# A mixture-of-experts stage whose experts are ranked by their count of tokens, with passes of 96 and 32 rows

## The chip, the cores and the metric

The kernel runs on one core of a Trainium2 chip. The metric is the device time of one execution in microseconds (us). Everything is float32; the matrix products of the experts are plain float32 matmuls.

## What is computed

The program is a stack of transformer layers. What matters here is the routed feed-forward layer, which occurs twice (layer l = 0 and 1), on 256 tokens of width 1024. The router picks for each token one group of four experts and two experts in that group, so 512 (token, expert) pairs fall on 16 experts:

```python
def hier_moe(x, w_rg, b_rg, w_re, b_re, w_gate, w_up, w_down):
    g_prob = jax.nn.softmax((t @ w_rg).astype(jnp.float32) + b_rg, axis=-1)
    g_val, g_idx = lax.top_k(g_prob, 1)
    ...
    e_val, e_idx = lax.top_k(e_logits, EXPERT_TOPK)
    e_w = jax.nn.softmax(e_val, axis=-1)
    ...
    for g in range(G):
        hg = jax.nn.silu(jnp.einsum('td,edf->tef', t, w_gate[g])) * jnp.einsum('td,edf->tef', t, w_up[g])
        y = y + jnp.einsum('tef,efd->td', hg * combine[:, g, :, None], w_down[g])
```

Each expert has three weight tiles of 2 MB (gate, up: 1024x512; down: 512x1024). The reference's router, evaluated on the inputs that setup_inputs() draws, gives these counts of tokens for experts 0 to 15:

| layer | counts |
|---|---|
| 0 | 46 53 20 25 31 60 39 24 14 43 50 29 16 20 13 29 |
| 1 | 11 8 4 13 77 33 111 69 27 33 14 24 18 17 20 33 |

## The kernel before

**Passes.** The chosen tokens of an expert are gathered into rows of a 128-row block. A pass handles one block, which two experts share: expert 2p has rows 0 to 63 and expert 2p + 1 rows 64 to 127. Eight passes (0 to 7) cover the sixteen experts with 64 rows each. An expert with more than 64 tokens gets further "items" of 64 rows, appended behind; two items share a pass. The number of passes, `pairs`, is half of (16 + items), rounded up, and is computed on the chip (`pairs_i`). With the counts above layer 0 has 8 passes. In layer 1 expert 4 needs one item, expert 6 one and expert 7 one: three items, 10 passes.

**One pass on TensorE** (`pair`): 32 program matmuls at L1607 for gate and up (8 slices k of the width, two products, two experts), `scatter` of the previous pass (L1589, 16 matmuls), four transposes (L1653), `gather` of the next pass's tokens (L1600), and 16 program matmuls at L1607 for down. The helper `both` issues at each step k one matmul for rows 0 to 63 and one for rows 64 to 127. The stationary operand is the tokens (64 columns), the moving one 512 columns of the expert's weights, so the two matmuls use two halves of the array's columns. Each program matmul in float32 appears in the trace as two weight loads and two matmuls. I call one (64, 64) pair of program matmuls a k-step; a pass has 8 + 8 + 8 = 24.

**VectorE and ScalarE** turn the products: `hs` = silu(gate) * up (L2795, once a pass, right behind up), the one-hot tables for the next gather (L2726, L2730), and the scaled result (L2809).

**The weights** come through eight slots of 2 MB: 0 to 5, and slots 6 and 7 (named `ahead_a` and `arena` in the trace), which hold the gate tiles of every other pass. SyncE (SP) issues the loads in the order gates of pass p + 1, up of p, down of p; each waits until TensorE has read what is in the slot (`pe_read`). The loads of passes 0 to 6 have addresses that are known when the program is built (L978). From pass 7 on they are in a loop whose addresses come from `expert_i` (L1000, L1006). The loads of the first eight tiles are issued before the layer's routing is known.

**Routing** is a chain of small VectorE instructions (`experts(l)` of the vector engine, L2681 to L2732), each waiting for the one before (`link`). It gives every chosen pair its row (`gp`), the one-hot table `oh`, on which TensorE's first gather waits, and, later, `pairs_i` and `expert_i`.

Of the kernel before, what the change touches and what calls it, by code (L numbers as in the profile page):

```python
# [31 lines left out]
I32 = mybir.dt.int32  # L32
# [5 lines left out]
P = 128  # L38
# [25 lines left out]
for _name, _w in [("ident", 128), ("ones", 128), ("blk64", 128), ("rotq", 128), ("dup0", 128), ("rot0", 128),  # L64
                  ("dup1", 128), ("rot1", 128), ("rotm", 128), ("before", 128), ("iota", 128), ("cosb", T0),
                  ("sinb", T0), ("maskt", TW), ("decay", RET_H * REAL), ("cosr", REAL), ("sinr", REAL), ("cosm", REAL),
                  ("sinm", REAL), ("causal", 384), ("over", OVER), ("first64", EXPERTS), ("over64", EXPERTS),
                  ("pairs", PAIRS), ("part", 1), ("last", 2), ("ones48", 48), ("sooner", 16), ("place", 8), ("thirds", 3),
                  ("windows", PAIRS + 1)]:
    CONST[_name] = (_at, _at + _w)  # L70
    _at += _w
# [18 lines left out]
def constants():  # L90
# [4 lines left out]
    def put(name, a):  # L95
        c[:, CONST[name][0]:CONST[name][1]] = a
# [46 lines left out]
    put("thirds", np.broadcast_to(HALF * np.arange(1, 4), (P, 3)))  # L143
    put("windows", np.broadcast_to(P * np.arange(PAIRS + 1), (P, PAIRS + 1)))
    put("over", np.broadcast_to(np.arange(OVER), (P, OVER)))
    put("first64", np.broadcast_to(HALF * np.arange(EXPERTS), (P, EXPERTS)))
    put("over64", np.broadcast_to(HALF * (EXPERTS - 1 - np.arange(EXPERTS)), (P, EXPERTS)))
    put("pairs", np.broadcast_to(2 * np.arange(PAIRS), (P, PAIRS)))
    put("part", p)
    put("last", np.broadcast_to(np.array([EXPERTS - 2, EXPERTS - 1]), (P, 2)))  # L150
    put("ones48", 1.0)

    rel = np.arange(-(T0 - 1), T0)
# [7 lines left out]
def program(nc, A, out, dbg=None):  # L161
# [510 lines left out]
    def area(n, *dims, at=None):  # L672

        a = pos[0] if at is None else at
        if at is None:
            pos[0] += n
        assert a + n <= ARENA, (a, n)
        v = arena[:, a:a + n]
        if len(dims) == 2:
            v = v.rearrange("p (a b) -> p a b", a=dims[0])  # L680
        if len(dims) == 3:
            v = v.rearrange("p (a b c) -> p a b c", a=dims[0], b=dims[1])
        if len(dims) == 4:
            v = v.rearrange("p (a b c d) -> p a b c d", a=dims[0], b=dims[1], c=dims[2])
        return v
# [114 lines left out]
    npf = area(1)  # L800
    assert pos[0] <= RANK_AT and AHEAD_AT + TILE <= EXPERT_AT, pos[0]

    expert_i = sb("expert_i", [1, 2 + OVER], I32)
# [133 lines left out]
    def _(sp):  # L937
# [29 lines left out]
            return (6, 7) if p % 2 else (0, 3)  # L967

        def load_experts(l):
            held = uses["moe", l, "tiles"]  # L970

            def take_slot(s):

                sp.wait_ge(*(tile_free(held[s]) if s < DENSE_SLOTS else (psum_full, read[segment_end[l] - 1])))
# [12 lines left out]
            for p in range(1, EXPERTS // 2 - 1):  # L987
                if p < EXPERTS // 2 - 2:
                    sp.wait_ge(moe[l]["pe"], p * 6 + pe_read[0])
                    for x in range(2):  # L990
                        load_tile(gate_slots(p + 1)[x], 6 * (p + 1) + 3 * x)
                for w in (1, 2):
                    sp.wait_ge(moe[l]["pe"], p * 6 + pe_read[w])
                    for x in range(2):
                        load_tile(3 * x + w, 6 * p + 3 * x + w)
            sp.wait_ge(route_ready, l + 1)
            sp.wait_ge(item_ready, l + 1)
            pairs = sp.value_load(pairs_i[0:1, 0:1], min_val=EXPERTS // 2, max_val=PAIRS)
            with sp.Fori(EXPERTS // 2 - 1, pairs) as p:
                e = [sp.value_load(expert_i[0:1, bass.ds(p * 2 + (x - EXPERTS + 2), 1)], min_val=0, max_val=EXPERTS - 1)  # L1000
                     for x in range(2)]
# [120 lines left out]
    def _(pe):  # L1122
# [441 lines left out]
        def experts(l):  # L1564
# [69 lines left out]
            def pair(p, gates, gate_loads):  # L1634

                pe.wait_ge(M["xe_act"], p + 1)
                pe.wait_ge(M["xe_dve"], p + 1)
# [2 lines left out]
                for g in range(2):  # L1640
                    if g == 1:
                        for x in range(2):
                            pe.wait_ge(moe_w[l][3 * x + 1], p * 16 + 16)
                    w = [slot(s) for s in (gates if g == 0 else (1, 4))]
                    for k in range(KC):
                        mm = both(w, g, xe, k, slice(0, 512), k == 0, k == KC - 1)
# [561 lines left out]
    def _(v):  # L2208
# [453 lines left out]
        def experts(l):  # L2662
            M = moe[l]
            v.tensor_copy(rank_w[:, 0, :], const("before"))
            v.tensor_copy(rank_w[:, 1, :], const("ones")).then_inc(rank_w_ready, 1)
            v.memset(more[:, 0:1], 0.0)
            v.wait_ge(small_loaded, 48)
            o = full(("logit", l))
            v.tensor_scalar(rtok, o[:, 40:42], 1.0 / D, EPS, ALU.mult, ALU.add).then_inc(rtok_sq, 1)
# [20 lines left out]
            for kk in range(2):  # L2690
# [16 lines left out]
            v.tensor_tensor(t16, rank, const("first64").unsqueeze(1).to_broadcast([P, 2, 16]), ALU.add)  # L2707
# [3 lines left out]
            link(v.scalar_tensor_tensor(out=base16, in0=begin16, scalar=float(HALF), in1=const("over64"), op0=ALU.mult,  # L2711
                                        op1=ALU.add))
            link(v.scalar_tensor_tensor(out=over16, in0=rank, scalar=float(HALF),
                                        in1=base16.unsqueeze(1).to_broadcast([P, 2, 16]), op0=ALU.is_ge, op1=ALU.mult))
            link(v.tensor_tensor(t16, t16, over16, ALU.add))
            link(v.tensor_tensor(picked, m16, t16.unsqueeze(1).to_broadcast([P, 2, 2, 16]), ALU.mult))
# [49 lines left out]
            v.tensor_copy(expert_i[0:1, 0:2], const("last")[0:1, :])  # L2766
            v.tensor_copy(expert_i[0:1, 2:], itemf[0:1, :]).then_inc(item_ready, 1)
# [199 lines left out]
```

## Time and profile before

| | |
|---|---|
| median of 3 runs | 1610.75 us (1609.91 to 1611.47) |
| the profiled execution | 1611.8 us, of which the span of the trace is 1610.0 us |
| mean granted TensorE clock | 0.97 of full speed |
| busy | PE 1501.8 us (93%), DVE 820.7 (51%), ACT 594.5 (37%), POOL 175.0 (11%) |
| matmuls at L1607 | 1728 records in 18 passes (8 of layer 0, 10 of layer 1) |
| first pass to end of last pass | 919.6 to about 1151 us (layer 0), 1308.8 to about 1592 us (layer 1) |
| loads of expert tiles | 108 of 2048 KB |

PE is TensorE's matmuls, PEld its weight loads (they overlap PE), DVE VectorE, ACT ScalarE. A matmul record's end is modelled; starts are measured. In a timeline row "x4" means that four records of one kind are merged, from the start of the first to the end of the last. A bracket gives the idle time of the engine before the row and what ended it.

### The profile page before, as it was taken

The page shows a single profiled execution, that of the slowest core. Times are in us where ns is not written, and L with a number is a line of the kernel's source. Part 1 is how long each engine was busy: PE and PEld are TensorE (multiplying, and loading weights), DVE is VectorE, ACT ScalarE, POOL GpSimd, SP SyncE. Part 2 cuts the span into 40 slices and gives each one's busy share as a digit, 9 for nine tenths or more (in the row PEclk, how much of TensorE's full clock was granted, in tenths as well). Part 3 has the DMA queues.
Part 4 walks back from the last instruction along what each step waited for, and adds up shares of the span by engine and source line. Part 5 has one row for each costly group of instructions (what it writes and reads, how often), then busy time and mean ns, then how long its engine had stood idle before and what let it go on. Part 6 is the DMA issues. An engine that isn't in the chain of part 4 may idle for free.

```text
span 1610.0 us, 25077 instructions
## 1 busy us (share of the span) xinstructions
PE 1501.8 (93%) x9938; PEld 1154.3 (72%) x9938; DVE 820.7 (51%) x1439; ACT 594.5 (37%) x1032; POOL 175.0 (11%) x171
## 2 busy tenths in 40 slices
PE   7998899998999999989999899899899989999996
PEld 6775899997679999888989754454676864444544
DVE  6876676677766656785557412111564532111213
ACT  4565544444664444534544211111433421111111
POOL 1000432242004332300000000000200000000000
PEclk9997999999999999999999899999899989999998
DMA  9041554544134545425511899999723189998993
GB/s 393 12 158 53 190 210 166 200 157 157 54 138 157 198 169 208 157 106 210 204 59 53 366 394 429 429 398 394 304 105 158 62 365 421 428 428 364 429 428 125
DMA packets 28760, 379.78 MB, mean 236 GB/s; under 512 B 3446, under 2 KB 4854, under 8 KB 5760
## 3 DMA queue, kind: packets, MB, share of 16 engines
q1 hardware_dynamic: 27312, 373.92, 57.9%
q0 software_dynamic: 928, 4.30, 0.7%
q8 instruction: 62, 1.02, 0.2%
q10 hardware_dynamic: 432, 0.32, 0.1%
q14 instruction: 26, 0.21, 0.0%
HBM read 377.45 MB, written 1.09 MB: 235 GB/s over the span
## 4 chain that ended last, share of the span: by engine, by line
PE 74%; DMA 11%; DVE 9%; ACT 3%; issue 1%; POOL 1%; SPq 0%; DVEq 0%; ACTq 0%; POOLq 0%
PE psum L1607 17%; PE psum L1140 13%; PE psum L1142 12%; PE psum L1141 12%; DMA ring<-w_expert_dram 11%; PE psum L1600 3%; PE psum L1162 2%; PE psum L1589 2%; DVE weight_low L2233 1%; PE psum L1500 1%; PE psum L1498 1%; PE psum L1499 1%; PE psum L1428 1%; PE psum L1418 1%; DMA ring<-w_dense_dram 1%
## 5 line engine op out<-in xcount | busy, mean ns | idle before, releaser
L1140 PE MATMUL psum<-x_high,weight_low 128*128 128x256 f32 (+1 forms) x1184 | 351.8, 297 | 31.6 <-DVE weight_low L2233 13.0
L1141 PE MATMUL psum<-x_low,weight_high 128*128 128x256 f32 (+1 forms) x1184 | 341.7, 289 | 0.0
L1142 PE MATMUL psum<-x_high,weight_high 128*128 128x256 f32 (+1 forms) x1184 | 341.7, 289 | 0.0
L2233 DVE TENSOR_TENSOR weight_low<-ring,weight_high 128x1024 fp32r<-128x1024 f32 x196 | 254.8, 1308 | 119.7 <-ACT weight_high L1796 119.2
L1796 ACT ACTIVATE weight_high<-ring 128x1024 fp32r<-128x1024 f32 x196 | 205.1, 1053 | 160.6 <-PE psum L1142 132.3
L1140 PEld LDWEIGHTS psum<-x_high,weight_low 128*128 128x128 f32 x1184 | 228.7, 193 | 49.6 <-issue 16.8
L1141 PEld LDWEIGHTS psum<-x_low,weight_high 128*128 128x128 f32 x1184 | 228.6, 193 | 1.2 <-issue 0.7
L1142 PEld LDWEIGHTS psum<-x_high,weight_high 128*128 128x128 f32 x1184 | 229.3, 194 | 0.0
L1607 PE MATMUL psum<-ring,xn 128*64 128x512 f32 x832 | 185.8, 602 | 18.3 <-DMA ring<-w_expert_dram 17.9
L1607 PEld LDWEIGHTS psum<-ring,xn 128*64 128x64 f32 x832 | 65.1, 139 | 136.4 <-issue 136.2
L1140 PE MATMUL psum<-hidden_high,weight_low 128*128 128x272 f32 (+1 forms) x512 | 145.8, 285 | 1.3 <-DVE hidden_low L2455 1.3
L1141 PE MATMUL psum<-hidden_low,weight_high 128*128 128x272 f32 (+1 forms) x512 | 145.8, 285 | 0.0
L1142 PE MATMUL psum<-hidden_high,weight_high 128*128 128x272 f32 (+1 forms) x512 | 145.5, 284 | 0.0
L1607 PE MATMUL psum<-ring,arena 128*64 128x512 f32 x576 | 127.6, 595 | 0.0
L2795 DVE TENSOR_TENSOR arena<-arena,psum 128x512 f32<-128x512 f32 x18 | 12.4, 688 | 218.0 <-PE psum L1607 218.0
L2447 DVE TENSOR_TENSOR weight_low<-ring,weight_high 128x1024 fp32r<-128x1024 f32 x64 | 87.2, 1362 | 60.7 <-ACT weight_high L1969 60.7
L1140 PEld LDWEIGHTS psum<-hidden_high,weight_low 128*128 128x128 f32 x512 | 96.2, 188 | 1.6 <-DVE hidden_low L2455 1.6
L1142 PEld LDWEIGHTS psum<-hidden_high,weight_high 128*128 128x128 f32 x512 | 96.7, 189 | 0.0
L1141 PEld LDWEIGHTS psum<-hidden_low,weight_high 128*128 128x128 f32 x512 | 96.5, 188 | 0.0
L1086 POOL TENSOR_TENSOR xn<-xn 128x256 f32<-128x256 f32 (+1 forms) x35 | 34.9, 997 | 536.0 <-ACT xn L1832 502.9
L1607 PEld LDWEIGHTS psum<-ring,arena 128*64 128x64 f32 x576 | 39.8, 137 | 74.1 <-issue 72.0
L1969 ACT ACTIVATE weight_high<-ring 128x1024 fp32r<-128x1024 f32 x64 | 67.7, 1058 | 57.5 <-PE psum L1142 57.5
(352 smaller groups left out, 2395.6 us busy)
## 6 DMA issues: line engine op xcount, KB each, us to landing
ring<-w_expert_dram SPq DMA_DIRECT2D x88, 2048.0 KB, 14.6
ring<-w_dense_dram SPq DMA_DIRECT2D x68, 2048.0 KB, 7.8
ahead_a<-w_expert_dram SPq DMA_DIRECT2D x10, 2048.0 KB, 15.4
arena<-w_expert_dram SPq DMA_DIRECT2D x10, 2048.0 KB, 19.7
arena<-scratch_dram POOLq DMA_DIRECT2D x1, 3328.0 KB, 12.8
constants_sb<-constants_dram SPq DMA_DIRECT2D x1, 1287.5 KB, 7.7
hT<-x_dram SPq DMA_DIRECT2D x1, 1088.0 KB, 5.3
constants_sb<-constants_dram SPq DMA_DIRECT2D x1, 1056.0 KB, 16.0
```

Of the source, the lines that this page charges most:

```text
L1086: pool.tensor_tensor(part[:, 0, :], part[:, 0, :], part[:, c, :], ALU.add).then_inc(folded, 1)
L1140: pe.matmul(o, wl[:, c % 4, cols], high, start=start, stop=False)
L1141: pe.matmul(o, wh[:, c % 4, cols], low, start=False, stop=False)
L1142: return pe.matmul(o, wh[:, c % 4, cols], high, start=False, stop=stop)
L1162: mm = pe.matmul(o[0:b - a, 0:n], x[:, k, a:b], w[:, k, first:first + n], start=(k == 0), stop=(k == KC - 1))
L1589: mm = pe.matmul(psum[:, 4 + c // 2, REAL * (c % 2):REAL * (c % 2) + REAL], part[:, c * P:(c + 1) * P], oht[:, :], start=False, stop=done ...
L1600: mm = pe.matmul(psum[:, c // 4, P * (c % 4):P * (c % 4) + P], xnat[:, tt, c * P:(c + 1) * P], oh[:, tt, :], start=(tt == 0), stop=(tt == 1))
L1607: mm = pe.matmul(psum[HALF * x:HALF * x + HALF, bank, :], x_[:, k, HALF * x:HALF * x + HALF], w[x][:, k, cols], start=start, stop=stop)
L1796: act.activation(split_view(wh, (name, j), c), quarter_view((name, j), q), ACT.Copy).then_inc(wh_ready, 1)
L1969: act.activation(split_view(wh, key, m["quarter"] + x), quarter_view(key, x % 4), ACT.Copy).then_inc(wh_ready, 1)
L2233: v.tensor_tensor(split_view(wl, (name, j), c), quarter_view((name, j), q), split_view(wh, (name, j), c).bitcast(F32), ALU.subtract).then_ ...
L2447: v.tensor_tensor(split_view(wl, key, c), quarter_view(key, x % 4), split_view(wh, key, c).bitcast(F32), ALU.subtract).then_inc(wl_ready, 1)
```

## The change

The experts 0 to 3 keep 64 rows each, in passes 0 and 1. The experts 4 to 15 are ranked on the chip by their counts. The five largest (ranks 0 to 4) get 96 rows, ranks 5 and 6 get 64, and ranks 7 to 11 get 32. Passes 2 to 6 ("wide") hold one 96-row expert (rows 0 to 95) and one 32-row expert (rows 96 to 127), pass 7 holds ranks 5 and 6. Further items of 64 rows start where an expert's own room ends. With the counts above all experts of layer 0 fit, and in layer 1 only expert 6 (111 tokens, 96 rows) needs an item: 8 and 9 passes.

In a wide pass `both` issues three matmuls at each step instead of two, of 64, 32 and 32 stationary columns. The routing chain gets the ranking, and SP reads expert numbers from `expert_i` for all loads from the gates of pass 2 on.

```diff
+WIDE = 96
+FIXED = 4
+RANKED = EXPERTS - FIXED
+BY_PLACE = (7, 8, 9, 10, 11, 0, 1, 2, 3, 4, 5, 6)
...
-            for p in range(1, EXPERTS // 2 - 1):
-                if p < EXPERTS // 2 - 2:
-                    sp.wait_ge(moe[l]["pe"], p * 6 + pe_read[0])
-                    for x in range(2):
-                        load_tile(gate_slots(p + 1)[x], 6 * (p + 1) + 3 * x)
-                for w in (1, 2):
-                    sp.wait_ge(moe[l]["pe"], p * 6 + pe_read[w])
-                    for x in range(2):
-                        load_tile(3 * x + w, 6 * p + 3 * x + w)
...
             sp.wait_ge(route_ready, l + 1)
             sp.wait_ge(item_ready, l + 1)
             pairs = sp.value_load(pairs_i[0:1, 0:1], min_val=EXPERTS // 2, max_val=PAIRS)
+            for p in range(1, EXPERTS // 2 - 1):
+                if p < EXPERTS // 2 - 2:
+                    n = p + 1 - FIXED // 2
+                    e = [sp.value_load(expert_i[0:1, i:i + 1], min_val=FIXED, max_val=EXPERTS - 1) for i in (5 + n, 4 - n)]
+                    sp.wait_ge(moe[l]["pe"], p * 6 + pe_read[0])
+                    for x in range(2):
+                        load_ranked(gate_slots(p + 1)[x], e[x], 0)
...
-            def both(w, bank, x_, k, cols, start, stop):
-
-                for x in range(2):
-                    mm = pe.matmul(psum[HALF * x:HALF * x + HALF, bank, :], x_[:, k, HALF * x:HALF * x + HALF],
-                                   w[x][:, k, cols], start=start, stop=stop)
+            def both(w, bank, x_, k, cols, start, stop, wide):
+
+                for x, a, b in ((0, 0, HALF), (0, HALF, WIDE), (1, WIDE, P)) if wide else ((0, 0, HALF), (1, HALF, P)):
+                    mm = pe.matmul(psum[a:b, bank, :], x_[:, k, a:b], w[x][:, k, cols], start=start, stop=stop)
                 return mm
...
-            with pe.Fori(0, EXPERTS // 4 - 1) as i:
-                pair(i * 2, (0, 3), i * 16 + 16)
-                pair(i * 2 + 1, (6, 7), i * 16 + 16)
-            pair(EXPERTS // 2 - 2, (0, 3), EXPERTS // 4 * 16)
+            pair(0, (0, 3), 16)
+            pair(1, (6, 7), 16)
+            with pe.Fori(1, EXPERTS // 4 - 1) as i:
+                pair(i * 2, (0, 3), i * 16 + 16, True)
+                pair(i * 2 + 1, (6, 7), i * 16 + 16, True)
+            pair(EXPERTS // 2 - 2, (0, 3), EXPERTS // 4 * 16, True)
...
-            link(v.tensor_tensor(more48.rearrange("p (e n) -> p e n", e=16), counts.unsqueeze(2).to_broadcast([P, 16, 3]),
-                                 const("thirds").unsqueeze(1).to_broadcast([P, 16, 3]), ALU.is_gt))
...
+            link(v.scalar_tensor_tensor(out=key12, in0=counts[:, FIXED:], scalar=float(EXPERTS), in1=const("tie"),
+                                        op0=ALU.mult, op1=ALU.add))
+            twelve = [P, RANKED, RANKED]
+            link(v.tensor_tensor(ahead12, key12.unsqueeze(1).to_broadcast(twelve), key12.unsqueeze(2).to_broadcast(twelve),
+                                 ALU.is_gt))
+            link(v.tensor_reduce(rank12, ahead12, AX.X, ALU.add))
+            link(v.tensor_tensor(held12, rank12.unsqueeze(2).to_broadcast(twelve),
+                                 const("by_place").unsqueeze(1).to_broadcast(twelve), ALU.is_equal))
+            link(v.tensor_tensor(looked, held12.unsqueeze(1).to_broadcast([P, 3, RANKED, RANKED]),
+                                 const("given", 3)[:, :, FIXED:].unsqueeze(2).to_broadcast([P, 3, RANKED, RANKED]), ALU.mult))
+            link(v.tensor_reduce(places[:, :, FIXED:], looked, AX.X, ALU.add))
+            first16, room16, delta16 = places[:, 0, :], places[:, 1, :], places[:, 2, :]
+            link(v.tensor_tensor(excess, counts, room16, ALU.subtract))
+            link(v.tensor_tensor(more48.rearrange("p (e n) -> p e n", e=16), excess.unsqueeze(2).to_broadcast([P, 16, 3]),
+                                 const("steps").unsqueeze(1).to_broadcast([P, 16, 3]), ALU.is_gt))
+            v.tensor_tensor(t16, rank, first16.unsqueeze(1).to_broadcast([P, 2, 16]), ALU.add)
+            v.tensor_tensor(beyond16, rank, room16.unsqueeze(1).to_broadcast([P, 2, 16]), ALU.subtract)
...
             link(compare(gp))
             link(one_hots(gp))
+            link(v.tensor_tensor(held12, held12, const("expert").unsqueeze(2).to_broadcast(twelve), ALU.mult))
+            link(v.tensor_reduce(placed, held12.rearrange("p e r -> p r e"), AX.X, ALU.add))
+            v.tensor_copy(expert_i[0:1, 0:RANKED], placed[0:1, :])
```

The program's order on TensorE, at the turn from down to the gates of an odd pass (slots 6 and 7, in rows `ahead_a` and `arena`), before (`both` is L1607):

```order
L1607 MATMUL psum<-ring,arena 64x512 x16
L1607 MATMUL psum<-ahead_a,xn 64x512
L1607 MATMUL psum<-arena,xn 64x512
L1607 MATMUL psum<-ahead_a,xn 64x512
L1607 MATMUL psum<-arena,xn 64x512
```

and of the changed kernel at the same place in a wide pass (`both` is L1645; the first number of a shape is the count of stationary columns):

```order
L1645 MATMUL psum<-ring,arena 64x512
L1645 MATMUL psum<-ring,arena 32x512 x2
L1645 MATMUL psum<-ahead_a,xn 64x512
L1645 MATMUL psum<-ahead_a,xn 32x512
L1645 MATMUL psum<-arena,xn 32x512
L1645 MATMUL psum<-ahead_a,xn 64x512
L1645 MATMUL psum<-ahead_a,xn 32x512
L1645 MATMUL psum<-arena,xn 32x512
```

What moved: between two 64-column matmuls there now stand two 32-column ones in place of one of 64; 24 such steps in each of the passes 2 to 6.

On VectorE, in the routing chain between the logits' difference and the scan over items, before:

```order
L2700 TENSOR_TENSOR arena<-arena 128x2
L2705 TENSOR_TENSOR arena<-psum,constants_sb 128x48
L2707 TENSOR_TENSOR arena<-psum,constants_sb 128x32
L2708 SCALAR_TENSOR_TENSOR arena<-constants_sb,arena 128x48
L2711 SCALAR_TENSOR_TENSOR arena<-arena,constants_sb 128x16
```

and of the changed kernel there:

```order
L2740 TENSOR_TENSOR arena<-arena 128x2
L2745 SCALAR_TENSOR_TENSOR arena<-psum,constants_sb 128x12
L2748 TENSOR_TENSOR arena<-arena 128x144
L2750 TENSOR_REDUCE arena<-arena 128x12
L2751 TENSOR_TENSOR arena<-arena,constants_sb 128x144
L2753 TENSOR_TENSOR arena<-arena,constants_sb 128x432
L2755 TENSOR_REDUCE arena<-arena 128x3x12
L2757 TENSOR_TENSOR arena<-psum,arena 128x16
L2758 TENSOR_TENSOR arena<-arena,constants_sb 128x48
L2760 TENSOR_TENSOR arena<-psum,arena 128x32
L2761 TENSOR_TENSOR arena<-psum,arena 128x32
L2762 SCALAR_TENSOR_TENSOR arena<-constants_sb,arena 128x48
```

What moved: seven linked instructions and one unlinked stand ahead of what was there.

## Rows read from the trace of the kernel before

**Rows 1.** The page, chain that ended last: share of the span by line.

```profile
PE psum L1607 17%; PE psum L1140 13%; PE psum L1142 12%; PE psum L1141 12%; DMA ring<-w_expert_dram 11%; PE psum L1600 3%; PE psum L1162 2%; PE psum L1589 2%; DVE weight_low L2233 1%; PE psum L1500 1%; PE psum L1498 1%; PE psum L1499 1%; PE psum L1428 1%; PE psum L1418 1%; DMA ring<-w_dense_dram 1%
```

**Rows 2.** Line L1607: records, duration ns min/median/max, first and last start us.

```profile
L1607 PE MATMUL psum<-ring,arena x576: 592/592/644, 939.6 to 1591.2; 128*64 128x512 f32 x192
```

**Rows 3.** Timeline of VectorE, line L2795, once a pass: start us, us, what.

```profile
960.51 0.69 DVE L2795 TENSOR_TENSOR arena<-arena,psum 128x512 f32<-128x512 f32 x1 [10.50 <-PE psum L1607]
987.38 0.69 DVE L2795 TENSOR_TENSOR arena<-arena,psum 128x512 f32<-128x512 f32 x1 [10.54 <-PE psum L1607]
...
1077.03 0.69 DVE L2795 TENSOR_TENSOR arena<-arena,psum 128x512 f32<-128x512 f32 x1 [14.73 <-PE psum L1607]
...
1376.58 0.69 DVE L2795 TENSOR_TENSOR arena<-arena,psum 128x512 f32<-128x512 f32 x1 [10.63 <-PE psum L1607]
...
1466.21 0.69 DVE L2795 TENSOR_TENSOR arena<-arena,psum 128x512 f32<-128x512 f32 x1 [14.83 <-PE psum L1607]
...
1519.96 0.69 DVE L2795 TENSOR_TENSOR arena<-arena,psum 128x512 f32<-128x512 f32 x1 [10.65 <-PE psum L1607]
...
1578.69 0.69 DVE L2795 TENSOR_TENSOR arena<-arena,psum 128x512 f32<-128x512 f32 x1 [13.15 <-PE psum L1607]
```

**Rows 4.** Timeline of PE in pass 0 of layer 1.

```profile
1308.84 13.95 PE L1607 MATMUL psum<-ring,xn 128*64 128x512 f32 x64
...
1325.17 3.74 PE L1600 MATMUL psum<-arena 128*128 128x128 f32 x32
1328.84 7.09 PE L1607 MATMUL psum<-ring,arena 128*64 128x512 f32 x32
```

**Rows 5.** The chain that ended last, layer 1: start us, us, what.

```profile
1376.94 21.59 DMA ring<-w_expert_dram
...
1398.67 7.10 PE psum L1607 x32
...
1457.39 8.78 PE psum L1607 x32
```

**Rows 6.** Timeline of PE: the two matmuls of a k-step, records by record.

```profile
1340.48 0.59 PE L1607 MATMUL psum<-ahead_a,xn 128*64 128x512 f32 x1
1340.48 0.59 PE L1607 MATMUL psum<-arena,xn 128*64 128x512 f32 x1
1340.91 0.59 PE L1607 MATMUL psum<-ahead_a,xn 128*64 128x512 f32 x1
```

**Rows 7.** Timeline of PEld where L1607 (64 columns) follows L1600 (128 columns).

```profile
1328.84 0.20 PEld L1607 LDWEIGHTS psum<-ring,arena 128*64 128x64 f32 x4
1329.32 0.14 PEld L1607 LDWEIGHTS psum<-ring,arena 128*64 128x64 f32 x2 [0.29 <-issue]
1329.75 0.14 PEld L1607 LDWEIGHTS psum<-ring,arena 128*64 128x64 f32 x2 [0.29 <-issue]
```

**Rows 8.** Timeline of PE where L1589 (128 columns) follows L1607 (64 columns).

```profile
1348.63 1.03 PE L1607 MATMUL psum<-ring,xn 128*64 128x512 f32 x4
1349.59 0.39 PE L1589 MATMUL psum<-slot_token,results_low 128*128 128x256 f32 x1
```

**Rows 9.** Timeline of PEld at L1428, another stage: 64 columns, 128 then 16 rows.

```profile
412.99 0.63 PEld L1428 LDWEIGHTS psum<-arena 128*64 128x64 f32 x8 [0.22 <-issue]
414.01 0.19 PEld L1428 LDWEIGHTS psum<-arena 16*64 16x64 f32 x4 [0.39 <-issue]
```

**Rows 10.** Timeline of VectorE and PE in the routing of layer 1.

```profile
1292.47 0.33 DVE L2681 TENSOR_TENSOR arena<-arena 128x160 f32<-128x160 f32 x1
...
1293.19 0.32 DVE L2683 TENSOR_REDUCE arena<-arena 128x40 f32<-128x160 f32 x1
...
1296.32 0.18 DVE L2711 SCALAR_TENSOR_TENSOR arena<-arena,constants_sb 128x16 f32<-128x16 f32 x1
...
1298.90 6.56 PE L1600 MATMUL psum<-arena 128*128 128x128 f32 x32 [3.57 <-DVE arena L2730]
...
1301.77 0.69 DVE L2758 TENSOR_TENSOR arena<-constants_sb,arena 128x512 f32<-128x512 f32 x1
```

More of the change, by code:

```diff
@@ L66 @@
                   ("sinb", T0), ("maskt", TW), ("decay", RET_H * REAL), ("cosr", REAL), ("sinr", REAL), ("cosm", REAL),
-                  ("sinm", REAL), ("causal", 384), ("over", OVER), ("first64", EXPERTS), ("over64", EXPERTS),
-                  ("pairs", PAIRS), ("part", 1), ("last", 2), ("ones48", 48), ("sooner", 16), ("place", 8), ("thirds", 3),
+                  ("sinm", REAL), ("causal", 384), ("over", OVER), ("tie", RANKED), ("by_place", RANKED), ("expert", RANKED), ("given", 3 * EXPERTS),
+                  ("pairs", PAIRS), ("part", 1), ("ones48", 48), ("sooner", 16), ("place", 8), ("steps", 3),
                   ("windows", PAIRS + 1)]:
@@ L142, in constants @@
     put("place", np.broadcast_to((four[None, :] - 3 + np.arange(2)[:, None]).reshape(1, 8), (P, 8)))
-    put("thirds", np.broadcast_to(HALF * np.arange(1, 4), (P, 3)))
+    put("steps", np.broadcast_to(HALF * np.arange(3), (P, 3)))
     put("windows", np.broadcast_to(P * np.arange(PAIRS + 1), (P, PAIRS + 1)))
     put("over", np.broadcast_to(np.arange(OVER), (P, OVER)))
-    put("first64", np.broadcast_to(HALF * np.arange(EXPERTS), (P, EXPERTS)))
-    put("over64", np.broadcast_to(HALF * (EXPERTS - 1 - np.arange(EXPERTS)), (P, EXPERTS)))
+    put("tie", np.broadcast_to(-np.arange(RANKED), (P, RANKED)))
+    put("by_place", np.broadcast_to(np.array(BY_PLACE), (P, RANKED)))
+    put("expert", np.broadcast_to(FIXED + np.arange(RANKED), (P, RANKED)))
+    first, room = np.zeros(EXPERTS, f), np.zeros(EXPERTS, f)
+    first[:FIXED], room[:FIXED] = HALF * np.arange(FIXED), HALF
+    for at, r in enumerate(BY_PLACE):
+        if r < 5:
+            first[FIXED + at], room[FIXED + at] = P * (FIXED // 2 + r), WIDE
+        elif r < 7:
+            first[FIXED + at], room[FIXED + at] = P * (EXPERTS // 2 - 1) + HALF * (r - 5), HALF
+        else:
+            first[FIXED + at], room[FIXED + at] = P * (FIXED // 2 + 11 - r) + WIDE, P - WIDE
+    given = np.stack([first, room, HALF * EXPERTS - room - first])
+    put("given", np.broadcast_to(given.reshape(1, -1), (P, 3 * EXPERTS)))
     put("pairs", np.broadcast_to(2 * np.arange(PAIRS), (P, PAIRS)))
     put("part", p)
-    put("last", np.broadcast_to(np.array([EXPERTS - 2, EXPERTS - 1]), (P, 2)))
     put("ones48", 1.0)
@@ L791, in program @@
     base16 = area(16)
+    key12, rank12 = area(RANKED), area(RANKED)
+    places = area(3 * EXPERTS, 3, EXPERTS)
+    excess = area(16)
+    beyond16 = area(32, 2, 16)
+    ahead12 = mdoh[:, 0:2, :].rearrange("p a b -> p (a b)")[:, 0:RANKED * RANKED].rearrange("p (a b) -> p a b", a=RANKED)
+    held12 = mdoh[:, 2:4, :].rearrange("p a b -> p (a b)")[:, 0:RANKED * RANKED].rearrange("p (a b) -> p a b", a=RANKED)
+    looked = eq4.rearrange("p a b -> p (a b)")[:, 0:3 * RANKED * RANKED].rearrange("p (k a b) -> p k a b", k=3, a=RANKED)
+    placed = area(RANKED)
     more48 = area(48)
@@ L801, in program @@
     assert pos[0] <= RANK_AT and AHEAD_AT + TILE <= EXPERT_AT, pos[0]
-    expert_i = sb("expert_i", [1, 2 + OVER], I32)
+    expert_i = sb("expert_i", [1, RANKED + OVER], I32)
     pairs_i = sb("pairs_i", [1, 1], I32)
@@ L969, in load_experts @@
         def load_experts(l):
-            held = uses["moe", l, "tiles"]
+            dense = uses["moe", l, "tiles"]
             def take_slot(s):
-                sp.wait_ge(*(tile_free(held[s]) if s < DENSE_SLOTS else (psum_full, read[segment_end[l] - 1])))
+                sp.wait_ge(*(tile_free(dense[s]) if s < DENSE_SLOTS else (psum_full, read[segment_end[l] - 1])))
             def load_tile(s, row):
@@ L986, in load_experts, with load_ranked, load_rest @@
                 load_tile(6 + x, 6 + 3 * x)
-            for p in range(1, EXPERTS // 2 - 1):
-                if p < EXPERTS // 2 - 2:
-                    sp.wait_ge(moe[l]["pe"], p * 6 + pe_read[0])
-                    for x in range(2):
-                        load_tile(gate_slots(p + 1)[x], 6 * (p + 1) + 3 * x)
+            def load_ranked(s, e, w):
+                sp.dma_start(expert_slot(s), A["w_expert"][l, bass.ds(e * 3 + w, 1), :, :].rearrange("a p n -> p (a n)")
+                             ).then_inc(moe_w[l][s], 16)
+            def load_rest(p, load):
                 for w in (1, 2):
@@ L994, in load_experts @@
                     for x in range(2):
-                        load_tile(3 * x + w, 6 * p + 3 * x + w)
+                        load(3 * x + w, x, w)
             sp.wait_ge(route_ready, l + 1)
@@ L998, in load_experts @@
             pairs = sp.value_load(pairs_i[0:1, 0:1], min_val=EXPERTS // 2, max_val=PAIRS)
+            for p in range(1, EXPERTS // 2 - 1):
[5 more added lines that the diff above has]
+                        load_ranked(gate_slots(p + 1)[x], e[x], 0)
+                if p == 1:
+                    load_rest(p, lambda s, x, w: load_tile(s, 6 * p + 3 * x + w))
+                else:
+                    load_rest(p, lambda s, x, w: load_ranked(s, held[x], w))
+                held = e
             with sp.Fori(EXPERTS // 2 - 1, pairs) as p:
-                e = [sp.value_load(expert_i[0:1, bass.ds(p * 2 + (x - EXPERTS + 2), 1)], min_val=0, max_val=EXPERTS - 1)
+                e = [sp.value_load(expert_i[0:1, bass.ds(p * 2 + (x - FIXED), 1)], min_val=0, max_val=EXPERTS - 1)
                      for x in range(2)]
@@ L1632, in experts, with pair @@
             pairs = pe.value_load(pairs_i[0:1, 0:1], min_val=EXPERTS // 2, max_val=PAIRS)
-            def pair(p, gates, gate_loads):
+            def pair(p, gates, gate_loads, wide=False):
                 pe.wait_ge(M["xe_act"], p + 1)
@@ L1645, in pair @@
                     for k in range(KC):
-                        mm = both(w, g, xe, k, slice(0, 512), k == 0, k == KC - 1)
+                        mm = both(w, g, xe, k, slice(0, 512), k == 0, k == KC - 1, wide)
                     mm.then_inc(M["pe"], 1)
@@ L2666, in experts @@
             v.memset(more[:, 0:1], 0.0)
+            v.tensor_copy(places[:, :, 0:FIXED], const("given", 3)[:, :, 0:FIXED])
             v.wait_ge(small_loaded, 48)
@@ L2710, in experts @@
             end16 = more[:, 1:49].rearrange("p (e n) -> p e n", e=16)[:, :, 2]
-            link(v.scalar_tensor_tensor(out=base16, in0=begin16, scalar=float(HALF), in1=const("over64"), op0=ALU.mult,
+            link(v.scalar_tensor_tensor(out=base16, in0=begin16, scalar=float(HALF), in1=delta16, op0=ALU.mult,
                                         op1=ALU.add))
-            link(v.scalar_tensor_tensor(out=over16, in0=rank, scalar=float(HALF),
+            link(v.scalar_tensor_tensor(out=over16, in0=beyond16, scalar=0.0,
                                         in1=base16.unsqueeze(1).to_broadcast([P, 2, 16]), op0=ALU.is_ge, op1=ALU.mult))
@@ L2765, in experts @@
             link(v.tensor_scalar(itemf, itemf, float(EXPERTS - 1), None, ALU.min))
-            v.tensor_copy(expert_i[0:1, 0:2], const("last")[0:1, :])
-            v.tensor_copy(expert_i[0:1, 2:], itemf[0:1, :]).then_inc(item_ready, 1)
+            v.tensor_copy(expert_i[0:1, RANKED:], itemf[0:1, :]).then_inc(item_ready, 1)
             v.tensor_copy(rowp, full(("rows", l)).rearrange("p (k t) -> p k t", k=2)).then_inc(dve_drained, 1)
```

3 lines of the change are left out of this document (1 added, 2 removed).

## The prediction

> **What bounds the kernel now.** I read the chain that ended last first, because the change touches only the two expert layers: L1607, the matmuls of `both`, holds 17% of the span and the loads of expert tiles another 11% [rows 1]. So both matter in this stage, and the question is which one sets a pass. VectorE's L2795 runs once a pass, right behind up, and is a good ruler: from one such row to the next is one pass. It gives 26.87 us for passes 1 to 2 of layer 0 (960.51 to 987.38) [rows 3]. That is all TensorE: 13.95 us gate and up, 3.74 gather, 7.09 down, the rest scatter and transposes [rows 4]. Other passes take longer: the three from 987.38 to 1077.03 take 89.65 us, which is 9.04 more than 3 x 26.87 = 80.61, and the three of layer 1 from 1376.58 to 1466.21 take 89.63, 9.02 more [rows 3]. There the chain goes through a tile on its way (21.59 us) before TensorE's 7.10 us of up, and once those 32 matmuls take 8.78 instead of 7.10 [rows 5]. So a pass costs 26.9 us when TensorE sets it and 29 to 31 when the weights do. The last two intervals, 1519.96 to 1578.69, take 58.73 [rows 3].
>
> **Passes that go.** By the counts of the reference's router, layer 0 keeps 8 passes, and layer 1 goes from 10 to 9, because experts 4 (77 tokens) and 7 (69) fit into 96 rows and only expert 6 (111) does not. One pass of about 29.4 us is gone; its matmuls, its six loads and its work on VectorE and ScalarE go together.
>
> **The wide passes** are the term that decides. A k-step is now two program matmuls of 64 columns side by side. The trace shows them truly at once: two records start at 1340.48, from `ahead_a` and from `arena`, and the next two 0.43 us later [rows 6]. Each program matmul has two such records, so a k-step takes 2 x 0.43 = 0.86 us; 16 steps of gate and up are 13.8 of the 13.95 us in [rows 4]. The wide step has three: 64, 32 and 32 columns, on disjoint columns of the array. No row of the trace shows matmuls of two widths side by side, so I bound the step from both sides. Lower end: all three at once, 0.86 us, as the two do now [rows 6]. A gain below that is excluded, since the 64-column matmul alone has its two records of 0.43. Upper end: one after another, 3 x 0.86 plus two changes of width.
>
> What a change of the array's shape costs is in the trace. From 64 to 128 columns: four records end at 1349.66 (1348.63 + 1.03), and with 0.59 us a record [rows 2] the last pair starts at 1349.07; the next matmul starts at 1349.59, 0.52 us later instead of 0.43, its weight load not ahead of it but beside it [rows 8]. From 128 to 64 columns: loads at 1328.84, then 1329.32, then 1329.75 [rows 7], so the first pair behind a change takes 0.48 instead of 0.43, for the second pair's load comes late too. And with 64 columns kept and only the rows changed from 128 to 16, the loads pause again: 8 loads end at 413.62, the next come at 414.01 [rows 9]. Every change of shape that the trace has lets the old work end (0.09 us more) and exposes a load (0.05 more). I take it that 64 to 32 is such a change too. Then the 32s cannot start until the 64 is through, and the next 64 not until the 32s are; only the two 32s share their time. A wide step: 0.48 + 0.52 for the 64, 0.48 + 0.52 for the two 32s, together 2.00 us, against 0.86: 1.14 us more.
>
> The Trainium skill says the same as a rule, in TensorEngine Tiling (Array Packing), Key Properties: changing the tiling mode, not just the tile, drains TensorE, and it lists 128x64 and 128x32 as different modes. The same section says that tiles work independently, and TensorE: Matmul & The Clock Gate, Part 3, gives 2.38 times for three 32-column matmuls packed together; by that figure alone, an estimate, three calls of 0.86 would take 1.08 us a step, and the sum below would come to about 1620 us. The trace agrees with the drain wherever the shape changes; no row here shows the mixed packing.
>
> Steps: 24 in a pass, 5 wide passes, 2 layers, 240 steps x 1.14 = +273.6 us, all on the path, because TensorE sets these passes alone: a wide pass takes 26.87 + 27.4 = 54.2 us, and six tiles need some 29.4. **What that hides**: the waits for tiles and the slow stretch go: -9.04 and -9.02. Behind pass 6 the loads are ahead, so the interval of pass 7 to 8 of layer 1 is 26.87; the two of 58.73 become one of 26.87: -31.86. In sum -49.9 us, the lost pass included.
>
> **The ranking** stands ahead of the first gather, for which TensorE waits 3.57 us on VectorE (L2730) now [rows 10]; nothing else is late there (the eight tiles are asked for before). Seven linked instructions: two tiny ones like L2711 (0.21 from start to start), three of 144 elements like L2681 and L2683 (0.36 each), a product of 432 elements and a reduction of 432. These lie between 0.33 for 160 elements and 0.69 for 512 [rows 10], so 0.64 each with the link. 0.42 + 1.08 + 1.28 = 2.8, and the unlinked `beyond16` 0.1: 2.9 us a layer, 2.3 to 3.5 by the two ends, +5.8 us in all. The three instructions behind `one_hots` (0.9 us) delay the table `dg`, but TensorE is in its gather for 6.56 us then [rows 10]: nothing. Without that cover they would cost 1.8 us.
>
> **SP's loads with addresses from memory.** SP now waits for `item_ready` before the gates of pass 2, and reads two numbers ahead of each pass's wait. The first of these loads is due only when the gates of pass 0 are read, 7 us into the pass, and the numbers are written before the pass begins. Queued behind on SP are only the loads of the same layer. In wide passes TensorE is late, so any fraction of a microsecond is hidden; if the weights set the passes, at most 1 or 2 us.
>
> **The sum.** 273.6 - 49.9 + 5.8 = +229.5 us. Against the profiled execution's 1611.8: 1841.3. The median is 1.05 below that execution, so 1840 us.
>
> **Rivals.**
> *Everything overlaps* (the other side, faster): the array's columns are what counts, the 64 and the 32s start together, a step stays at 0.86. For it: each half of the array has its own order already (the second expert's first record starts before the first expert's second, although it is issued later) [rows 6]. Against it: the pause at every change of shape [rows 7 to 9]. Then the waits for tiles stay and one pass goes: -29.4 + 5.8 = -23.6, 1587 us. The sign turns at a small price: the passes have 49.9 - 5.8 = 44.1 us to give, over 240 steps 0.18 us a step. Below a step of 1.04 us the change gains, above it loses.
> *No pause, but no overlap of 64 with 32*: step 1.72, +0.86 x 240 = 206.4, total 1610.75 + 206.4 - 44.1 = 1773 us. Against it: the 0.09 and 0.05 us in [rows 7 to 9].
> *Nothing overlaps, or the clock falls*: three in a row with two changes, 2.58 + 0.28 = 2.86, +2.00 x 240: 2047 us. With half the array idle the granted clock could drop for long; the 32 matmuls of the gather take 6.56 us behind an idle stretch and 3.74 in a pass [rows 4, 10]. At half clock throughout, a step would be 3.7 us and the total near 2250. Against it: apart from a stretch like the 8.78 one, TensorE at work in this stage takes 7.1 us for 32 matmuls every time [rows 4, 5].
> *The change doesn't drop the pass*: should the chip's counts differ from the reference's, layer 1 keeps 10 passes, +26.9 on the forecast, 1867 us. The 18 passes of the trace fit the reference's counts exactly, so I give this 1 in 100.
>
> **How the numbers follow.** Forecast (drain at each change) 66%, everything overlaps 24%, no pause 4%, nothing overlaps or half clock 5%, pass stays 1%. The forecast's own range is 1820 to 1875: 0.06 us either way on the step is 14 us, the ranking 1, and ten stretches like the 8.78 one (1.7 us each) would add 17. As the fast case holds more than 2 in 10, the range reaches to it: 1584 to 1875. It leaves out 5 or 6 in 100. About 0.2% (3 us) is what a measurement of this kernel can tell from no change; only a step within 0.02 us of 1.04 would land there. Faster 0.24, same 0.01, slower 0.75.
>
> **What would show it.** In the trace of the changed kernel: L2795 from pass 3 to 4 some 54 us apart (26.9 to 29.4 if all overlap, 47.5 without the pause); in `both` at L1645 a 64-column record, 0.48 us, another, 0.52 us, then two 32-column ones starting together, and never a 32 inside a 64; no wait of TensorE for expert tiles in layer 0 behind pass 2; 17 rows of L2795's successor; the wait of the first gather near 6.5 us. The prediction is wrong if 32-column records start within a few nanoseconds of a 64-column one.

## The result and the profile after

The changed kernel takes 1832.14 us (median of 4 runs, 1828.95 to 1834.45), the kernel before beside it 1610.33: 1.138 times as long (95% interval 1.136 to 1.140). The prediction was 1840 us, slower, on the ground that a wide step's 64-column and 32-column matmuls do not share their time. The profiled execution took 1834.45 us, its span is 1832.6 us.

The page of the changed kernel, the chain that ended last by line:

```profile
PE 86%; DVE 9%; ACT 2%; issue 1%; DMA 1%; POOL 1%; SPq 0%; DVEq 0%; ACTq 0%; POOLq 0%
PE psum L1645 34%; PE psum L1178 11%; PE psum L1179 10%; PE psum L1180 10%; PE psum L1638 4%; PE psum L1627 2%; PE psum L1200 1%; DVE weight_low L2272 1%; PE psum L1537 1%; PE psum L1536 1%; PE psum L1538 1%; DMA ring<-w_dense_dram 1%; PE psum L1466 1%; PE psum L1456 1%; PE psum L1262 1%
```

`both` (now L1645) has gone from 17% of the chain [rows 1] to 34%, and the loads of expert tiles, 11% before, are no longer in the list. TensorE alone sets the stage.

VectorE's timeline, the line behind up, once a pass (L2851 answers to the L2795 of [rows 3]); passes 1 to 4 of layer 0, then 6, 7 and 8 of layer 1:

```profile
964.93 0.69 DVE L2851 TENSOR_TENSOR arena<-arena,psum 128x512 f32<-128x512 f32 x1 [10.60 <-PE psum L1645]
1009.68 0.69 DVE L2851 TENSOR_TENSOR arena<-arena,psum 128x512 f32<-128x512 f32 x1 [28.52 <-PE psum L1645]
1063.43 0.69 DVE L2851 TENSOR_TENSOR arena<-arena,psum 128x512 f32<-128x512 f32 x1 [28.68 <-PE psum L1645]
1117.18 0.69 DVE L2851 TENSOR_TENSOR arena<-arena,psum 128x512 f32<-128x512 f32 x1 [28.68 <-PE psum L1645]
...
1739.99 0.69 DVE L2851 TENSOR_TENSOR arena<-arena,psum 128x512 f32<-128x512 f32 x1 [28.68 <-PE psum L1645]
1775.87 0.69 DVE L2851 TENSOR_TENSOR arena<-arena,psum 128x512 f32<-128x512 f32 x1 [10.80 <-PE psum L1645]
1802.75 0.69 DVE L2851 TENSOR_TENSOR arena<-arena,psum 128x512 f32<-128x512 f32 x1 [10.65 <-PE psum L1645]
```

A whole wide interval is 53.75 us, to the hundredth the same from pass to pass (forecast 54.2), where [rows 3] had 26.9 to 31. The last, pass 7 to 8, is 26.88: the loads are ahead again. There are 17 such rows, one fewer than before, so layer 1 has its 9 passes.

Inside a wide step, timeline of PE. The number behind the star is the count of stationary columns:

```profile
1559.77 0.62 PE L1645 MATMUL psum<-ahead_a,xn 128*32 128x512 f32 x1
1559.78 0.62 PE L1645 MATMUL psum<-arena,xn 128*32 128x512 f32 x1
1560.22 0.59 PE L1645 MATMUL psum<-ahead_a,xn 128*32 128x512 f32 x1
1560.23 0.59 PE L1645 MATMUL psum<-arena,xn 128*32 128x512 f32 x1
1560.75 1.62 PE L1645 MATMUL psum<-ahead_a,xn 128*64 128x512 f32 x3
1561.76 0.62 PE L1645 MATMUL psum<-arena,xn 128*32 128x512 f32 x1
```

and of its weight loads:

```profile
1560.75 0.19 PEld L1645 LDWEIGHTS psum<-ahead_a,xn 128*64 128x64 f32 x2 [0.84 <-issue]
1561.75 0.11 PEld L1645 LDWEIGHTS psum<-ahead_a,xn 128*32 128x32 f32 x1 [0.81 <-issue]
1561.76 0.11 PEld L1645 LDWEIGHTS psum<-arena,xn 128*32 128x32 f32 x1
```

The two 32s start together (1559.77 and 1559.78), their second records 0.45 us later, and the 64 starts at 1560.75, 0.53 behind those. The row "x3" merges the two records of the 64 with the first 32 behind them, which starts with its load at 1561.75; so the next 32s come a full 1.0 us after the 64 (its two records, 0.48 and 0.52 us). One step is 1561.76 - 1559.77 = 1.99 us, 1.985 over several; before, it was 0.86 [rows 6]. The load of the first 32 starts with its matmul and not ahead of it. That is the pause of [rows 7 to 9], twice in every step.

The first gather now waits longer. PE's timeline in layer 1:

```profile
1429.99 6.21 PE L1638 MATMUL psum<-arena 128*128 128x128 f32 x32 [6.36 <-DVE arena L2784]
```

6.36 us instead of the 3.57 of [rows 10].

### The profile page after: what moved, and what is told of

It reads as the page before. It is cut to its first block, busy times and chain, and to the rows that moved or that the text cites. A ratio compares the mean times of both kernels' runs of the same rounds, so it can differ in the third digit from the quotient of the medians.

```text
span 1832.6 us, 25851 instructions
## 1 busy us (share of the span) xinstructions
PE 1737.4 (95%) x10270; PEld 1147.6 (63%) x10270; DVE 821.3 (45%) x1451; ACT 589.9 (32%) x1027; POOL 175.5 (10%) x171
## 4 chain that ended last, share of the span: by engine, by line
PE 86%; DVE 9%; ACT 2%; issue 1%; DMA 1%; POOL 1%; SPq 0%; DVEq 0%; ACTq 0%; POOLq 0%
PE psum L1645 34%; PE psum L1178 11%; PE psum L1179 10%; PE psum L1180 10%; PE psum L1638 4%; PE psum L1627 2%; PE psum L1200 1%; DVE weight_low L2272 1%; PE psum L1537 1%; PE psum L1536 1%; PE psum L1538 1%; DMA ring<-w_dense_dram 1%; PE psum L1466 1%; PE psum L1456 1%; PE psum L1262 1%
## 5 line engine op out<-in xcount | busy, mean ns | idle before, releaser
L1645 PE MATMUL psum<-ring,xn 128*64 128x512 f32 (+1 forms) x1056 | 317.8, 604 | 0.0
L1835 ACT ACTIVATE weight_high<-ring 128x1024 fp32r<-128x1024 f32 x196 | 205.3, 1054 | 160.4 <-PE psum L1180 132.0
L1179 PEld LDWEIGHTS psum<-x_low,weight_high 128*128 128x128 f32 x1184 | 229.5, 194 | 1.1 <-issue 0.7
L1645 PEld LDWEIGHTS psum<-ring,xn 128*64 128x64 f32 (+1 forms) x1056 | 63.6, 122 | 251.3 <-issue 251.2
L1645 PE MATMUL psum<-ring,arena 128*32 128x512 f32 (+1 forms) x704 | 209.1, 605 | 0.0
L2851 DVE TENSOR_TENSOR arena<-arena,psum 128x512 f32<-128x512 f32 x17 | 11.7, 688 | 364.9 <-PE psum L1645 364.9
L1645 PEld LDWEIGHTS psum<-ring,arena 128*32 128x32 f32 (+1 forms) x704 | 42.3, 123 | 153.6 <-issue 151.6
L2865 DVE SCALAR_TENSOR_TENSOR results_low<-psum,arena,results_high 128x1024 fp32r<-128x1024 f32 x17 | 21.8, 1284 | 197.7 <-ACT results_high L2185 197.7
L1645 PE MATMUL psum<-ahead_a,xn 128*64 128x512 f32 x208 | 99.0, 604 | 0.0
```

The source lines that it names most:

```text
L1179: pe.matmul(o, wh[:, c % 4, cols], low, start=False, stop=False)
L1645: mm = pe.matmul(psum[a:b, bank, :], x_[:, k, a:b], w[x][:, k, cols], start=start, stop=stop)
L1835: act.activation(split_view(wh, (name, j), c), quarter_view((name, j), q), ACT.Copy).then_inc(wh_ready, 1)
L2865: v.scalar_tensor_tensor(out=yel[:, :].rearrange("p (h n) -> p h n", h=2), in0=psum[:, 2:4, :], scalar=wcur[:, 0:1], in1=yeh[:, :].bitcast ...
```

## The experiments

Eight kernels ran. Each ratio is to the kernel before on the same chip: 1608.36 us beside the first four, 1609.16 beside the last four. Theory A: a change of width between 64 and 32 columns drains TensorE, that is, the matmuls under way end before one of the other width starts. The rivals: TensorE runs at most two matmuls at once (B), the extra weight loads cost (C), a third matmul costs, whatever its width (D), or the ranking and its addresses share in the loss.

**No change of width: four matmuls of 32.** On the changed kernel:

```diff
-for x, a, b in ((0, 0, HALF), (0, HALF, WIDE), (1, WIDE, P)) if wide else ((0, 0, HALF), (1, HALF, P)):
+for x, a, b in ((0, 0, 32), (0, 32, HALF), (0, HALF, WIDE), (1, WIDE, P)) if wide else ((0, 0, HALF), (1, HALF, P)):
```

> The changed kernel with its wide passes in four matmuls of 32 columns a step (the 64-column one split in two), so that no step has two widths. Theory A, a change of width between 64 and 32 columns drains TensorE: nothing changes width inside a step, the four run at once, a step is back at 0.86 us, a pass at 26.9 to 29.4, and the total is 1587 us, below the kernel before. Rival B, TensorE runs at most two matmuls at once whatever their widths: two pairs one after the other, a step of 1.72 us, a pass near 47.5, total about 1773. Rival C, each weight load of 32 columns (0.11 us in the changed kernel's records) queues behind the others: eight loads in 0.86 us, a step of about 0.9 to 1.0, total 1590 to 1610.

Measured: 1588.07 us, ratio to the kernel before 0.987 (0.985 to 0.990). More matmuls than in the changed kernel and 244 us less. PEld's timeline in a wide pass:

```profile
1056.74 0.13 PEld L1645 LDWEIGHTS psum<-ring,arena 128*32 128x32 f32 x4 [0.30 <-issue]
1057.17 0.13 PEld L1645 LDWEIGHTS psum<-ring,arena 128*32 128x32 f32 x4 [0.30 <-issue]
1057.60 0.13 PEld L1645 LDWEIGHTS psum<-ring,arena 128*32 128x32 f32 x4 [0.30 <-issue]
```

Four loads together every 0.43 us, so four matmuls of one width share their time as two of 64 columns do, and a step is 0.86 us. The loads of weight tiles set some passes again, 15 us of waiting in all (us in total, times, longest):

```profile
PE psum L1645 <- DMA ring<-w_expert_dram: 14.8, 9, 2.5
```

B falls, and the step leaves no room for C, which is tested more closely below; A stands. This version is faster than the kernel before by 1.3%, with an interval that excludes none.

**Few changes of width: all 64s of a product, then its 32s.**

```diff
-                    for k in range(KC):
-                        mm = both(w, g, xe, k, slice(0, 512), k == 0, k == KC - 1, wide)
+                    for part in ((0, 1) if wide else (None,)):
+                        for k in range(KC):
+                            mm = both(w, g, xe, k, slice(0, 512), k == 0, k == KC - 1, wide, part)
```

with the same in down; part 0 is the 64-column matmul, part 1 the two of 32.

> The changed kernel with each product's 64-column matmuls issued first for all its steps, and its 32-column pairs behind them: 6 changes of width in a wide pass instead of 48 or so, no overlap of 64 with 32. Theory A (drain at each change, 0.14 us each): 24 steps take 24 x 1.72 + 6 x 0.14 = 42.1 us instead of 24 x 1.985 = 47.6, a wide pass 48.2 instead of 53.75, total 1777 us. If the pause at a change costs nothing and the order alone keeps them apart, the time stays at 1832. If the 32s could run inside the 64s when they are queued in long rows, a step falls to 0.86 and the total towards 1590.

Measured: 1779.41 us (ratio 1.106, 1.103 to 1.109), wide intervals:

```profile
1541.01 0.69 DVE L2854 TENSOR_TENSOR arena<-arena,psum 128x512 f32<-128x512 f32 x1 [24.92 <-PE psum L1646]
1589.13 0.69 DVE L2854 TENSOR_TENSOR arena<-arena,psum 128x512 f32<-128x512 f32 x1 [24.92 <-PE psum L1646]
```

48.12 us (48.2 expected). So of the 26.88 us that a wide pass lost, 53.75 - 48.12 = 5.6 is the pauses (some 42 fewer, 0.13 us each) and 21.2 is what remains with hardly a pause, that is, the 64 and the 32s taking turns. Nearly four fifths of the price is the overlap lost, one fifth the pause. In this order the program itself keeps the 64s and the 32s apart, so it prices the pause; that they do not overlap when they stand side by side is shown by the changed kernel's step above and by the two matmuls of unequal width below.

**Everything but the width.** The changed kernel with `for x, a, b in ((0, 0, HALF), (1, HALF, P)):` in every pass.

> The changed kernel with two matmuls of 64 columns in every pass; the rows 64 to 95 of a wide pass are multiplied with the small expert's weights, so that part of the result is left wrong. It has the ranking, the addresses from the ranking and the nine passes of layer 1, but not the third matmul. Theory A: all of the loss is in the third matmul; 1610.3 - 29.4 + 5.8 = 1587 us. Rival: the ranking chain or the loads with addresses from memory cost more than the 2.9 us a layer and are hidden in the slow passes; then 1590 to 1600.

Measured: 1586.03 us (ratio 0.986, 0.983 to 0.989). The ranking, the addresses and the dropped pass together give 22 us; the loss is all in `both`.

**The width alone.** The kernel before with

```diff
+                for x, a, b in ((0, 0, HALF), (1, HALF, 96), (1, 96, P)) if wide else ((0, 0, HALF), (1, HALF, P)):
+                    mm = pe.matmul(psum[a:b, bank, :], x_[:, k, a:b], w[x][:, k, cols], start=start, stop=stop)
```

> The kernel before with only the split: passes 2 to 6 of each layer in matmuls of 64, 32 and 32 columns, the two 32s with the second expert's weights; no ranking, 10 passes in layer 1, nothing left out. Theory A: 240 steps x 1.128 = +270.7 us, less the waits that the slow passes hide (9.04, 9.02 and 2.5 to 5 in passes 7 to 9 of layer 1): 1858 to 1861 us, wide passes 53.75 us apart. Rival: if part of the loss of the changed kernel came from the ranking or the addresses, this one is below 1850.

Measured: 1857.02 us (ratio 1.154, 1.151 to 1.158), just below the expected 1858 to 1861; wide intervals again 53.75:

```profile
1570.54 0.69 DVE L2796 TENSOR_TENSOR arena<-arena,psum 128x512 f32<-128x512 f32 x1 [28.68 <-PE psum L1607]
1624.29 0.69 DVE L2796 TENSOR_TENSOR arena<-arena,psum 128x512 f32<-128x512 f32 x1 [28.68 <-PE psum L1607]
```

**Two matmuls, but of unequal width.** As the last one, without `(1, 96, P)`.

> The kernel before with two matmuls a step in passes 2 to 6 as ever, but of 64 and 32 columns; rows 96 to 127 of these passes are left out, so the result lacks those tokens. Theory A (a change of width drains TensorE, whatever the number of matmuls): a step costs what the three cost, 1.985 us, wide passes 53.75 us apart, total about 1857 as with the full split. Rival D (what costs is the third matmul, that is more than two of unequal kind in flight): two matmuls on disjoint columns run at once, 0.86 us a step, passes 26.9 to 29.4, total about 1608.

Measured in a single run: 1855.81 us; wide intervals of 53.60:

```profile
1516.69 0.69 DVE L2796 TENSOR_TENSOR arena<-arena,psum 128x512 f32<-128x512 f32 x1 [28.39 <-PE psum L1607]
1570.29 0.69 DVE L2796 TENSOR_TENSOR arena<-arena,psum 128x512 f32<-128x512 f32 x1 [28.57 <-PE psum L1607]
```

and PE's timeline inside such a pass:

```profile
1554.83 3.55 PE L1607 MATMUL psum<-ring,xn 128*64 128x512 f32 x7
```

Seven records take 3.55 us, one after another; in pairs they would take about 1.9. Less work than the kernel before, and 26.7 us more per pass. Two matmuls on disjoint columns run at once when they are 64 and 64, and not at all when they are 64 and 32. The difference is far beyond the scatter of any kernel here (under 1%), so one run is enough. D falls: the third matmul is nearly free (0.15 us a pass), the width is what costs.

**Four 32s on the kernel before.** The line is `((0, 0, 32), (0, 32, HALF), (1, HALF, 96), (1, 96, P))` in passes 2 to 6.

> The kernel before with passes 2 to 6 in four matmuls of 32 columns a step, nothing left out, 10 passes in layer 1, no ranking. Theory A: four of one width cost what two of 64 cost, so the time is that of the kernel before within 0.2%: 1605 to 1612 us. Rival C (more weight loads a step cost something): above 1615. It also says what the dropped pass is worth: the difference to the changed kernel in four 32s should be 29.4 - 5.8 = 23.6 us less about 1 to 2 us for addresses from memory.

Measured: 1610.40 us beside 1609.16, ratio 1.001 (0.999 to 1.003). The finer split costs nothing that can be measured, and C falls. So what the changed kernel gains in four 32s, 1610.4 - 1587.5 (below) = 22.9 us, is its dropped pass less the ranking (23.6, less 1 to 2, was expected).

**Hiding the ranking.** On the four-32 version the one-hot table of pass 0 is made ahead of the ranking. Experts 0 to 3 have fixed rows; the others get 4096, which matches no row:

```diff
+            v.tensor_tensor(t16, rank, const("early").unsqueeze(1).to_broadcast([P, 2, 16]), ALU.add)
+            link(v.tensor_scalar(over16, rank, float(HALF), 4096.0, ALU.is_ge, ALU.mult))
+            link(v.tensor_tensor(t16, t16, over16, ALU.add))
+            link(v.tensor_tensor(picked, m16, t16.unsqueeze(1).to_broadcast([P, 2, 2, 16]), ALU.mult))
+            link(v.tensor_reduce(gp.rearrange("p t k -> p k t"), picked, AX.X, ALU.add))
...
+            link(compare(gp))
+            link(one_hots(gp))
             link(v.scalar_tensor_tensor(out=key12, in0=counts[:, FIXED:], scalar=float(EXPERTS), in1=const("tie"),
...
-            link(compare(gp))
-            link(one_hots(gp))
+            link(v.tensor_scalar(gpw, gp, -float(P), None, ALU.add))
```

> The changed kernel in four 32s, with the one-hot table of pass 0 (experts 0 to 3 have fixed rows) made before the ranking, so that TensorE's first gather does not wait for it. The wait of the first gather falls from 6.4 us to about 2.5. Behind it TensorE then waits for the scaled table of the slot weights, which VectorE finishes about 11.6 us behind the ranks instead of the 13.7 at which TensorE needs it today: 2 us a layer gained, 4 us in all, 1584 us. If that wait eats all of it, 1588; if the tables came in time, 7 us in all, 1581.

> The changed kernel in four matmuls of 32 columns once more, beside the early gather on the same chip: 1588 us, ratio to the kernel before 0.987 as the first time; it is the base against which the early gather's 4 us are read.

Measured: the early gather 1593.81 us (ratio 0.991, 0.989 to 0.993), the base beside it 1587.49 (0.987, 0.985 to 0.989). The edit lost some 6 us where 4 were expected as gain. Waits of PE in the early gather, us in total, times, longest:

```profile
PE psum L1639 <- DVE arena L2762: 5.4, 2, 2.7
...
PE psum L1661 <- DVEq L2824: 4.0, 2, 2.0
...
PE psum L1668 <- issue: 2.1, 2, 1.1
...
PE psum L1655 <- DVE arena L2801: 1.7, 2, 1.2
```

The first gather's wait fell to 2.7 us as expected, and the wait for the scaled table (L2824) is 2.0 us as expected. Two more were not in the expectation: 1.2 and 0.6 us for the table `dg` (L2801), which now also comes late, and 1.1 us instead of 0.4 ahead of L1668. So there are four waits in a row, and the clock fell in them. Stretches of layer 0 (us, PE busy, granted clock, DMA share, GB/s), the early gather from the end of its gather on:

```profile
918.40:926.70 8.30, 4.12 (x16) 0.81 1.00 428
926.70:932.00 5.30, 5.30 (x17) 0.65 0.42 178
```

and its base:

```profile
916.70:920.10 3.40, 2.97 (x18) 1.00 1.01 434
920.10:926.00 5.90, 5.90 (x29) 1.00 0.59 251
```

In the base the first pass begins at the full clock, in the early gather its first 5.3 us have 0.65, that is, much of them the lower of the two levels (1.2 GHz). In finer stretches the early gather's clock is 1.00 from 917.0 us, at the end of its gather, to 922.6, at the end of the wait of 2.0 us, 0.50 from 923.7 to 930.0, and 1.00 again from 932 on. In layer 1 the first pass's gate and up show it less, 14.50 us against 13.96. By parts, against the base: from the rank matmuls to the first gather 3.7 us less in each layer; from there to pass 0, where the waits stand, 5.1 and 4.4 us more; gate and up of pass 0 1.8 and 0.5 us more. From the rank matmuls to `hs` of pass 0 the early gather takes 32.6 and 31.3 us in the two layers, its base 29.4 and 30.1: +4.4 us of the 6.3. So what turned the expected gain into a loss is mostly the waits that were left out, some 3 us in both layers, and the low clock, some 4 us: the four records of L1668 took 2.05 us instead of 1.17, and pass 0's gate and up as above. The other 2 us stay open: the two profiled executions differ by 4.7 us in all, and in code that no edit touches by as much as that (the profiled executions reach the routing of layer 0 anywhere between 904.7 and 910.0 us).

## Why the prediction was right

Its sum by parts, in the profiled executions (a rise of the span by 222.6 us; 229.5 were forecast).

- **The step, "2.00 us, against 0.86".** It is 1.985: 0.48 + 0.52 for the 64 as taken from [rows 7, 8], then 0.45 + 0.53 for the 32s. A wide interval grew by 53.75 - 26.87 = 26.88 us, 1.12 a step: 268.8 in all for the forecast's 273.6. The size was taken 2% too large, mainly because the 32s' late load costs 0.02, not the 0.05 of a 64's.
- **"What that hides", -49.9.** First to last L2851 is 322.52 us in layer 0 and 349.39 in layer 1, where the kernel before had 197.14 and 255.86: +218.9. With the steps' 268.8 that makes -49.9, as forecast; no wait for an expert tile is left in the chain, and pass 7 to 8 takes 26.88.
- **The ranking, +5.8.** The first gather's wait grew by 2.8 us in each layer (3.57 to 6.36), the 2.9 of the chain. But only 1.9 and 2.2 us arrive at pass 0, +4.2 us in all, because the gather itself took 6.13 us instead of 6.73 in layer 0 and 6.21 instead of 6.56 in layer 1; its mean granted clock was 0.59 instead of 0.53, and 0.58 instead of 0.55. The prediction took the gather's time as fixed. That the longer wait shortened it is not shown: with the same wait of 6.4 us other kernels have anything from 5.22 to 6.59 us, so this part of the difference may be chance. The three instructions behind `one_hots` cost nothing, as said.
- **The rest** moved by -0.5 us: +2.5 ahead of the routing of layer 0, -1.5 between the two expert layers and -1.5 behind the last, all in code that the change does not touch.
- **The rivals.** "Everything overlaps" would have had 32-column records inside the 64; there is none, and the sign turned by far: 1.985 us is beyond the 1.04 at which the change breaks even. Its number, 1587 us, was right for the four-32 version (1588.07, 1587.49), in which everything does overlap. The step of "no pause, but no overlap" (1.72 us, 1773 in all) is what the grouped order has, at 1779 with its remaining pauses.
- **What both halves having their own order tells.** The prediction named it as the rival's support [rows 6]. It is true and not enough: matmuls of one width keep their own orders side by side, but matmuls of two widths take turns.

The Trainium skill says in TensorEngine Tiling (Array Packing), Key Properties, that changing the mode drains TensorE and that different tiles can run in parallel. The traces agree with both: 64 beside 32 takes turns (a step of 1.98 us), 64 beside 64 and four 32s run at once (0.86 us). The Trainium skill's 2.38 times for three packed 32-column matmuls (TensorE: Matmul & The Clock Gate, Part 3), by which the changed kernel's step would have been 1.08 us, an estimate, does not carry over to it: the step of 64, 32 and 32 took 1.985 us. Four matmuls in one mode do better than that figure, a step of 0.86 us, the time of one.

## What to carry to other kernels

When a block is split unevenly over the array's columns, cut every piece to the same width, even if it makes more matmuls: 32 + 32 + 32 + 32 cost what 64 + 64 cost, and 64 + 32 + 32 more than twice that. This is shown for float32, 128 rows and 512 moving columns; other types and shapes did not run. Before mixing shapes inside an inner loop, look in the trace at any place where shapes change and at whether the weight load runs ahead of its matmul there. And a wait that is shortened at one place is not gained if several short ones follow before a dense stretch: here they added up to more, and the clock fell in them and was still low when the stretch began.

## What the runs showed of the hardware that I had not expected

- Eight weight loads in 0.86 us, four at a time, cost nothing measurable: ratio 1.001 (0.999 to 1.003) against two of 64 columns with four loads.
- A 32-column load that is exposed by a change of width costs about 0.02 us, a 64-column one 0.05.
- The third matmul of a step, 32 columns beside another 32, adds 0.15 us to a pass of 53.6.
- The first gather of a layer, part of which runs at the low clock, took anything from 5.22 to 6.73 us, with no order by the wait ahead of it: 5.44 and 6.03 us behind 2.7 us, 5.44 to 6.73 behind 3.6, 5.22 to 6.59 behind 6.4. So a difference of half a microsecond there says nothing of an edit.
